# The expert stage's overflow branches nested, and the next stage's first transfers issued from inside the expert stage

## The reference

```python
hu = xb @ w_up[e] + b_up[e]                       # 1024 -> 2048
x_glu = jnp.minimum(hu[:, :D_FF], SWIGLU_LIMIT)
x_lin = jnp.clip(hu[:, D_FF:], -SWIGLU_LIMIT, SWIGLU_LIMIT)
act = x_glu * jax.nn.sigmoid(SWIGLU_ALPHA * x_glu) * (x_lin + 1.0)
y = act @ w_down[e] + b_down[e]                   # 1024 -> 1024
out = jax.ops.segment_sum(y * row_gate[:, None], row_tok, num_segments=T)
x = x + gate2 * out
```

```python
h, gate = adaln(x, mod)          # rmsnorm(x) * (1 + scale) + shift
hc, gate_c = adaln(xc, mod_c)    # xc = ctx_2
pp, ppc = h @ w_in, hc @ w_in    # w_in = ab_w_in_2, 1024 x 2336
```

## Time and profile before

| what | value |
|---|---|
| median of 3 runs | 3147.25 us (3146.09 to 3155.44) |
| the profiled execution's own time | 3151.83 us |
| its span | 3150.6 us |
| TensorE busy, share of the span | 87% |
| mean granted TensorE clock | 0.925 |

### The profile page before, as it was taken

The page is one execution under the profiler, slowest core; times in us unless marked ns, Lnnn a source line. Parts: engine busy times, 40 slices in busy tenths (PEclk is TensorE's granted clock), DMA queues, the critical chain, the costliest instruction groups (busy, mean ns, idle before and its releaser), DMA issues. The chain is left out here.

```text
span 3150.6 us, 25764 instructions
## 1 busy us (share of the span) xinstructions
PE 2753.3 (87%) x9523; PEld 1338.4 (42%) x9523; DVE 1021.6 (32%) x2160; ACT 568.9 (18%) x1280; POOL 175.5 (6%) x321
## 2 busy tenths in 40 slices
PE   6888868849999999999999990499899888999998
PEld 2534655433444444433444430255534334454443
DVE  3663444341111111111111110424265555232362
ACT  1354121000000000000000000211344344110240
POOL 0000442000000000000000000100000000000000
PEclk9989989859999999999999995699889889999899
DMA  8201385228999999589958981410100000121100
GB/s 296 73 38 54 125 305 228 94 109 333 395 398 381 403 352 394 221 331 397 417 204 315 390 328 48 162 54 24 54 0 1 1 27 1 34 73 62 52 1 27
DMA packets 142901, 567.14 MB, mean 180 GB/s; under 512 B 15477, under 2 KB 35182, under 8 KB 104738
## 3 DMA queue, kind: packets, MB, share of 16 engines
q1 hardware_dynamic: 126296, 515.45, 42.2%
q0 software_dynamic: 13712, 45.12, 3.8%
q10 hardware_dynamic: 2746, 4.61, 0.4%
HBM read 538.27 MB, written 26.87 MB: 179 GB/s over the span
## 5 line engine op out<-in xcount | busy, mean ns | idle before, releaser
L1565 PE MATMUL ps<-ring,mem 128*128 128x512 f32 (+1 forms) x1648 | 600.9, 600 | 1.4 <-issue 1.4
L214 PE MATMUL ps<-ring,mem 128*128 128x512 f32 (+5 forms) x1136 | 397.9, 508 | 47.0 <-DMA ring<-in_ab_w_in 15.7
L214 PE MATMUL ps<-mem,ring 128*128 128x512 f32 (+1 forms) x1056 | 422.2, 560 | 2.6 <-DVE mem L732 1.6
L1565 PEld LDWEIGHTS ps<-ring,mem 128*128 128x128 f32 (+1 forms) x1648 | 230.8, 168 | 309.0 <-issue 309.0
L220 PE MATMUL ps<-mem 128*128 128x128 f32 (+3 forms) x1243 | 203.5, 298 | 175.5 <-DVE mem L1914 108.8
L214 PEld LDWEIGHTS ps<-ring,mem 128*128 128x128 f32 x1136 | 203.3, 197 | 226.6 <-issue 191.6
L214 PEld LDWEIGHTS ps<-mem,ring 128*128 128x128 f32 x1056 | 201.7, 192 | 213.6 <-issue 204.8
L220 PEld LDWEIGHTS ps<-mem 128*128 128x128 f32 (+3 forms) x1243 | 154.5, 150 | 312.0 <-issue 155.0
L1594 PE MATMUL ps<-ring,mem 128*64 128x512 f32 (+1 forms) x736 | 252.4, 594 | 0.0
L1626 DVE COPY mem<-ps 128x512 f32<-128x512 f32 x52 | 36.0, 692 | 558.6 <-PE ps L220 558.6
L1565 PE MATMUL ps<-mem 128*64 128x512 f32 (+1 forms) x528 | 200.2, 600 | 0.0
(11 more groups left out here) (356 smaller groups left out, 2421.9 us busy)
## 6 DMA issues: line engine op xcount, KB each, us to landing
ring<-in_w_up SPq DMA_DIRECT2D x96, 2048.0 KB, 11.9
ring<-in_w_down SPq DMA_DIRECT2D x42, 2048.0 KB, 17.6
mem<-in_w_up SPq DMA_DIRECT2D x32, 2048.0 KB, 12.3
mem<-in_w_down SPq DMA_DIRECT2D x22, 2048.0 KB, 15.9
ring<-in_w_ada SPq DMA_DIRECT2D x12, 2048.0 KB, 7.4
ring<-in_mod_w SPq DMA_DIRECT2D x8, 2048.0 KB, 10.3
y_rows<-mem POOLq DMA_DIRECT2D x26, 512.0 KB, 7.9
ring<-in_cd_w_in SPq DMA_DIRECT2D x6, 2048.0 KB, 7.6
```

The source lines that it names most:

```text
L214: i = e.matmul(o, l, r, start=(n == 0), stop=(n == len(pairs) - 1))
L1565: m = e.matmul(PS[n][c0:c0 + rows, :], XGT[:, u, k * 128 + c0:k * 128 + c0 + rows], wt[:, kk, n * 512:n * 512 + 512], start=False, stop=(k ...
```

## The change

Four things are done, none of which changes what is computed.

1. The branches stand one inside the other. Behind the work of block j there is one short test for the end (`cnt == j + 1`), then the test for block j + 1, inside the body of block j's own test. With a number of zero, an engine's first test leads to the end of the whole nest.
2. The further blocks no longer use slots 0 to 4 of the ring but slots 3 to 6 (four slots), so slots 0 to 2 are free for the next layer.
3. The three first `load_next` of the layer move in front of the branches: SP issues them right behind the last tile of the experts, each once the slot's last expert tile is used.
4. The loads of the context and of the gate row move to the start of ACT's expert stage. They need room that the expert stage doesn't use, so `XC` and `GR` now lie just under `wide_at`, and other arrays of the layer are laid out anew (`HT` and `XN` over slots 5 and 6). The table `c3` is still loaded at the layer's start.

The diff, cut (the layout of later stages and the same rewriting for DVE, ACT and POOL are left out):

```diff
     for n, parts in enumerate(loads):
-        if n == n_first:
-            held = {}
         before[n] = held.get(slot_of(n), -1)
...
+    XC_at, GR_at = wide_at - 3072, wide_at - 1024
+    assert top[0] <= XC_at
+    XC, GR = alloc(2, 1024, at=XC_at), alloc(1024, at=GR_at)
+    d3, dgr = [dma_count(n) for n in ("late", "gate2")]
...
     def act_experts(e):
+        e.dma_start(XC, D["ctx_2"][0].rearrange("(t p) d -> p t d", p=128)).then_inc(*d3.up(16))
+        e.dma_start(GR, row(MOD[5120:6144])).then_inc(*dgr.up(16))
         for i in range(NMAIN):
             act_gate(e, main, i)
...
-    load_on(nc.sync, n_first)
+    load_on(nc.sync, n_first + 3)
     meet([(main.stored[0], 16 * (NMAIN - NMAIN // 2)), (main.stored[1], 16 * (NMAIN // 2))])
...
-            s = m % NSLOT
-            return ring[:, s * 4096:(s + 1) * 4096], (loaded_x[s], 16 * (m // NSLOT + 1))
+            return slot(3 + m % 4), (loaded_x[m % 4], 16 * (m // 4 + 1))
...
+    def each_extra(e, step):
+
+        cnt = extra_count(e)
+
+        def behind(j):
+            with e.If(cnt > j):
+                step(j)
+                with e.If(cnt == j + 1):
+                    extra_end(e, j)
+                if j + 1 < NXB:
+                    behind(j + 1)
+
+        behind(0)
+
     def pe_extras(e):
-        cnt = extra_count(e)
-        for j in range(NXB):
-            with e.If(cnt > j):
-                pe_turn_x(e, more, j, 0)
-                pe_turn_x(e, more, j, 1)
-                pe_up(e, more, j, x_parts(j), lambda q: None)
-                pe_turn_a(e, more, j, 0)
-                pe_turn_a(e, more, j, 1)
-                pe_down(e, more, j, x_parts(j))
-        for j in range(NXB):
-            with e.If(cnt == j + 1):
-                extra_end(e, j)
+        def step(j):
+            pe_turn_x(e, more, j, 0)
+            pe_turn_x(e, more, j, 1)
+            pe_up(e, more, j, x_parts(j), lambda q: None)
+            pe_turn_a(e, more, j, 0)
+            pe_turn_a(e, more, j, 1)
+            pe_down(e, more, j, x_parts(j))
+
+        each_extra(e, step)
...
-        e.dma_start(XC, D["ctx_2"][0].rearrange("(t p) d -> p t d", p=128)).then_inc(*d3.up(16))
-        e.dma_start(GR, row(MOD[5120:6144])).then_inc(*dgr.up(16))
         e.dma_start(c3, D["cst3"]).then_inc(*dc3.up(16))
...
-    for _ in range(3):
-        load_next(nc.sync)
     pe_layer1(nc.tensor)
```

More of the change, by code:

```diff
@@ L1514, in emit @@
     BU = alloc(NBU // 4 * 1536).bitcast(BF16).rearrange("p (a n) -> p a n", n=3072)
-    assert top[0] <= wide_at
+    XC_at, GR_at = wide_at - 3072, wide_at - 1024
+    assert top[0] <= XC_at
+    XC, GR = alloc(2, 1024, at=XC_at), alloc(1024, at=GR_at)
+    d3, dgr = [dma_count(n) for n in ("late", "gate2")]
     def bias_words(x):
@@ L1758, in emit @@
     pool_experts(nc.gpsimd)
-    load_on(nc.sync, n_first)
+    load_on(nc.sync, n_first + 3)
     meet([(main.stored[0], 16 * (NMAIN - NMAIN // 2)), (main.stored[1], 16 * (NMAIN // 2))])
     more = Lane("x")
-    loaded_x = [sem(f"ring_loaded_x{s}") for s in range(NSLOT)]
+    loaded_x = [sem(f"ring_loaded_x{s}") for s in range(4)]
     def x_parts(j):
@@ L1798, in dve_extras @@
-    def dve_extras(e):
[L1799 to L1809, removed]
-    def act_extras(e):
[L1812 to L1819, removed]
@@ L1821, in pool_extras @@
-    def pool_extras(e):
[L1822 to L1831, removed]
+    def each_extra(e, step):
[8 more added lines that the diff above has]
+        behind(0)
@@ new lines, in pe_extras, with step @@
+    def pe_extras(e):
+        def step(j):
[6 more added lines that the diff above has]
+        each_extra(e, step)
+    def dve_extras(e):
+        def step(j):
+            dve_copy_x(e, more, j, 0)
+            dve_copy_x(e, more, j, 1)
+            dve_swiglu(e, more, j)
+            dve_copy_a(e, more, j, 0)
+            dve_copy_a(e, more, j, 1)
+        each_extra(e, step)
@@ new lines, in act_extras, with step @@
+    def act_extras(e):
+        def step(j):
+            act_gate(e, more, j)
+            act_copy_y(e, more, j)
+        each_extra(e, step)
+    def pool_extras(e):
+        def step(j):
+            ex = e.value_load(XE[0:1, j:j + 1], min_val=0, max_val=NEXP - 1)
+            pool_gather(e, more, j, NMAIN + j)
+            pool_biases(e, more, j, BIASD[bass.ds(ex, 1)].rearrange("a k n -> (a k) n"), j - NBU if j >= NBU else None)
+            pool_store(e, more, j, NMAIN + j)
+        each_extra(e, step)
@@ L1835, in sp_extras, with step @@
             e.wait_ge(*f.now())
[L1836 to L1852, removed]
+        def step(j):
+            ex = e.value_load(XE[0:1, j:j + 1], min_val=0, max_val=NEXP - 1)
+            w1 = D["w_up"][0, bass.ds(ex, 1)].rearrange("a k n -> (a k) n")
+            w2 = D["w_down"][0, bass.ds(ex, 1)].rearrange("a k n -> (a k) n")
+            for q, parts in enumerate(up_loads(w1) + down_loads(w2)):
+                m = 6 * j + q
+                if m >= 4:
+                    j0, q0 = divmod(m - 4, 6)
+                    e.wait_ge(*((more.up, 4 * j0 + q0 + 1) if q0 < 4 else (more.down, 2 * j0 + q0 - 3)))
+                for dst, src in parts:
+                    e.dma_start(dst(slot(3 + m % 4)), src).then_inc(loaded_x[m % 4], 16)
+        each_extra(e, step)
     with nc.Block() as block:
@@ L1877, in emit @@
     top[0] = base
-    XC = alloc(2, 1024)
     mark = top[0]
-    c3 = alloc(640)
     GTE = alloc(8, 768)
@@ L1885, in emit @@
     GQ = alloc(6, 512)
[L1886 to L1890, removed]
+    c3 = alloc(640)
     rt = alloc(1024)
-    assert top[0] <= WORDS - 4096
+    assert top[0] <= XC_at
+    HT = alloc(8, 768, at=wide_at)
+    XN = alloc(2, 1024, at=wide_at + 6144)
+    ACC = mem[:, mark:mark + 2048].rearrange("p (a n) -> p a n", n=1024)
     sb = small[:, 32:48]
@@ L1899, in emit @@
     R = lambda at, *dims: spare[:, at:at + int(np.prod(dims))].rearrange("p (a n) -> p a n", n=dims[1])
-    d3, dgr, dc3 = [dma_count(n) for n in ("late", "gate2", "cst3")]
+    dc3 = dma_count("cst3")
     dyg = [dma_count(f"yg{k}") for k in range(8)]
@@ L2412, in emit @@
     PB, LK1 = [gq_[:, a * 1536:a * 1536 + 1536].rearrange("p (a n) -> p a n", n=768) for a in range(2)]
-    top[0] = tail - 6144
+    top[0] = GR_at
     LQ, LK, LV = [alloc(4, 768), R(0, 4, 768)], [[alloc(2, 768), alloc(2, 768)], [LK1, R(3072, 2, 768)]], [alloc(6, 256), GKV]
     QA, KA = alloc(2, 384), alloc(2, 384)
-    assert top[0] <= tail + 3072
+    assert top[0] <= WORDS - 4096
     m_latent, wl = take()
@@ L2578, in emit @@
     TM, XN = R(2048, 2, 512), R(3072, 2, 1024)
-    top[0] = mark + 640
+    top[0] = mark
     PQ = alloc(4, 512)
@@ L2582, in emit @@
     UP = alloc(4, 514)
-    top[0] = mark + 640 + 6144
+    top[0] = mark + 6144
     MT = alloc(8, 512)
-    HT = alloc(8, 768)
     YF = alloc(2, 512)
-    rt = alloc(1024)
     GR1 = alloc(1024)
-    assert top[0] <= WORDS - 4096, top[0]
+    assert top[0] <= mark + 14016
+    HT = alloc(8, 768, at=wide_at)
     dgl = dma_count("gate3")
```

## The result

| | before | changed |
|---|---|---|
| median | 3149.97 us (4 runs, 3146.09 to 3155.44) | 3068.53 us (4 runs, 3068.34 to 3072.76) |
| ratio | | 0.9743, 95% interval 0.9725 to 0.9762 |
| span of the profiled execution | 3150.6 us | 3067.2 us |

The change is 81.4 us in the medians where 74.9 were summed up; 2.7 us of this difference come from the median of the kernel before, which stood at 3147.25 when the forecast was made and at 3149.97 with a fourth execution.

The account below looks back on a forecast made before the run. TensorE is busy 87% of the span, so time comes back only where it idles, chiefly the 66 us gap behind the experts. -50.3 - 8.4 - 15.5 - 2.1 + 1.4 = -74.9 us from 3147.25 gave 3072.5 us, range 3064 to 3086.

Parts of the forecast that it names:

- The gap is set by PE's 16 long tests, one fetch each, 3.35 us: Idle stretch behind the experts: each failed long test fetches 16 KB; the nest removes 15 of 16 fetches, 50.3 us.
- The 4.3 us counted from the last fetch to 1960: End of the gap: one fetch period plus about 1 us for the 16 short tests and the barrier.
- One far jump stays with one fetch: Nest on PE: one jump past all bodies still costs one fetch; a second fetch would lower 50.3 to 46.9 us.
- The 108 ns for a compare-and-branch: Skill's figure for a test: by it alone 31 tests would be worth an estimated 3.3 us, the time near 3119.
- The context 8.4 us, the weights 15.5: Layer's start: early context moves ACT's square 8.4 us earlier, early weights the first product 15.5; together 23.9 us.
- The clock, 2.1 us: Layer's first products: without the wait they follow while the granted clock is 1.0, at half the time; 2.1 us less.
- The gather at the experts' start, +1.4 us: Experts' start: context and gate, 1.5 MB, loaded there delay the first gather by 1.4 us; bounds 0 and 3.9.
- The moved weight tiles cost nothing: End of the experts: the layer's three tiles, queued behind the last `w_down` tile, land before 1909.7 and cost 0.
- C: Rival: the gap hangs on the length of code skipped, so the nest gains nothing; 3122.7 us, chance 0.04.
- D: Rival: early loads gain nothing, the next wait ending as late as the removed one; 3098 us, chance 0.05.
- B: Rival: the far jump is dearer, 3 to 6 fetches, 6.7 to 16.8 us come back; 3079 to 3089, chance 0.08.
- The slower one: Rival E: early 1.5 MB costs SP's transfers their lead, stalling PE in eight two-expert blocks; slower than before, chance 0.02.

Follow-up runs that it names:

- a1: Changed kernel with the tests in a row again, as in the kernel before, early loads kept; 3124.91 us.
- b1: Kernel before with TensorE's part of the further blocks left out, its 16 long bodies cut to the block-end waits, all 32 tests kept; 3104.85 us.
- a3: Changed kernel with four nests of four blocks in a row in place of one nest of 16; 3089.72 us.
- a7: Changed kernel with two nests of eight blocks in a row in place of one nest of 16; 3078.48 us.
- d1: Changed kernel with the number of further blocks loaded on every engine before the engines wait for each other; 3073.30 us.
- d3: Changed kernel with the number loaded before the engines wait for each other and the last block's store issued by ACT; 3066.00 us.

## Why the prediction was right, step by step

- **The gap is set by PE's 16 long tests, one fetch each, 3.35 us: right.** a1 puts the whole 51 us back, b1 takes most of it away (46.4 us) with the tests left standing. Above the floor of 9.15 us the stage costs 56.7 us, 3.5 for each of the 16 with the number's load, the short tests and the barrier. (The 4.3 us counted from the last fetch to 1960 don't come out of the earlier trace rows, whose slice leaves 2.8 to 4.2; only a bound hung on them.)
- **"One far jump stays with one fetch": the count was wrong, the sum hardly.** A far jump brings two blocks, of which one lies in the gap and the second falls at the layer's start; each further one costs 5.1 to 5.4 us (a3, a7). The gap shrank by 51.3 us where 50.3 was taken: beyond the 15 fetches and the floor, 6.4 us were left standing, and the nest, with load, jump and barrier, uses 5.35 of them. With the 1.0 to 1.2 us of the number's load (d1, d3) taken off, I estimate the one jump and the barrier at 4.2 to 4.4 us. That the sum comes out within 1.0 us with a wrong count is in part luck. The rule of the Trainium skill ("Runtime: NRT & Kernel Launch", Instruction fetch mechanics), a fetch before anything can go on, was borne out, and its 16 KB block for PE; q14's packets are 8 KB. The 108 ns for a compare-and-branch ("Advanced Engine Details and Errata", Control Flow Timing), by which the time was put at an estimated 3119, doesn't hold for PE's long tests, at 3.4 us each. For tests whose target needs no fetch b1 gives only the bound of 0.32 us.
- **The context 8.4 us, the weights 15.5: the sum right, the shares not.** 23.9 was summed for the first product, and it came 24.0 earlier (31.7 to 7.8). Undone alone they are worth 4.6 and 20.9 to the first product, since each transfer was late partly because of the other: the context lands at 5.0 us in place of 9.0 without the weights beside it, and with the context early the product stands until 28.7 in place of 31.7.
- **The clock, 2.1 us: 1.6, and not for the reason given.** The 96 products take 24.93 us in place of 26.57. In the kernel before, the clock was up from 1976.0 on, while PE still turned the rows, and I took it that it would be so here. In the changed kernel it is still at 0.50 until 1912.0, when the turn is over and the product has begun. What is saved is that PE goes on without a wait and the clock rises early in the product, 0.84 over the 5 us from 1911, where it was 0.50 over those from 1991.
- **The gather at the experts' start, +1.4 us: mis-sized, 0.15.** 9.83 became 9.98 us to PE's first turn, and over all profiles the difference is 0.4. What the 1.5 MB delayed were the two `w_up` tiles, by 4.5 us, and nothing waited for them.
- **The moved weight tiles cost nothing: right.** First turn to last copy is 1199.7 in both.
- **The total.** 6.5 us more than forecast. The touched pieces gave 76.9 in place of 74.9: 1.0 more from the gap, 1.25 less lost at the gather, 0.4 less from the layer's start. In the profiled pair, 6.5 us more came from the two pieces outside the change, of which 4.9 before the experts, where the granted clock differed. How much of the medians' 81.4 is such luck can't be told from 4 runs each.

Of the rivals, C (the gap isn't from the tests' number) and D (another wait as late) are out by a1 and by the timeline. B, the dearer jump, was right in kind, with two blocks for a jump, but none of its 6.7 to 16.8 us came back: the gap ended 1.0 us shorter than summed. The slower one had no sign: the expert stage's DMA share is 0.89 and its length the same.

## What to carry to other kernels

A stage that does nothing can be the longest wait of a kernel: look in the page's slices for one where every engine is idle and then, in the DMA view, at the instruction queues. Code that is seldom run should be skipped by one jump, since each failed test that led out of the instructions at hand cost 3.4 to 5.4 us here on the engine with the longest bodies. And transfers that a stage needs first can be issued before such a gap, as soon as their room is free; what each is worth isn't the wait put down to it (15.7 us for the weights, which are worth 20.9), since they share the way.

## What the runs showed of the hardware

- PE's instructions come through q8 in packets of 16 KB (16 packets, 0.26 MB; 1 in b1). q14, which b1 leaves at 9 packets and 0.07 MB, carries packets of 8 KB; that these are the other four engines' follows by exclusion, no run shows it engine by engine.
- A jump past 4, 8 or 16 bodies brings two blocks on PE (8, 4 and 2 packets for 4, 2 and 1 jumps), and each further jump past 4 or 8 costs 5.1 to 5.4 us; one past a single body costs 3.4 us and brings one block. For the jump past 16, only an upper bound of 5.35 us is measured, with the number's load and the barrier in it.
- A drain on POOL right behind a store that it issued ends 7.4 us after the issue begins, 7.7 us after SP's wait on it does, while the store lands 2.9 us after its issue; with the store on ACT, the same gap is 4.95 us shorter.
- Identical instructions ahead of the experts take 678.4 to 688.0 us from execution to execution, and the time follows the granted clock of the stretch 240 to 260: 1.00 at 678.4 to 680.1 us, 0.72 at 688.0.
